# Adding tiles before their sums, turning the heads inside the pointwise product, and starting the convolution beside the second u product

## What is computed

```python
mod = c_act @ ada_w[l] + ada_b[l]                       # 6144 values: shift, scale, gate
h = rms_norm(x, norm_g[l]) * (1 + scale) + shift
z = h @ w_in[l]
q_lat, kv_lat, k_rope, mla_gate, conv_in, conv_gate = split(z)      # 512, 256, 64, 1024, 2048, 1024
q  = rms_norm(q_lat)  @ w_q_up[l]                       # 8 heads of 128 + 64
kv = rms_norm(kv_lat) @ w_kv_up[l]                      # 8 heads of 128 + 128
q, k = rms_norm over each head, then rope on the last 64 columns (k's 64 are shared by the heads)
mla_out = causal_attention(q, k, v) * silu(mla_gate)
u = u_val * sigmoid(u_gate)                             # from conv_in
u = causal_depthwise_conv(u, dw_w[l], dw_b[l])          # 31 taps, 1024 channels
u = silu(layer_norm(u)) @ w_pw[l] + b_pw[l]
conv_out = u * silu(conv_gate)
x = x + gate * (concat(mla_out, conv_out) @ w_out[l])
```

## Time and profile before

| | us |
|---|---|
| runs, median (lowest to highest) of 3 | 2267.42 (2266.95 to 2269.32) |
| the profiled execution, its own time | 2269.92 |
| its span | 2268.1 |
| PE busy | 2189.5 (97%) |
| DVE busy | 1672.6 (74%) |
| ACT busy | 975.8 (43%) |
| POOL busy | 221.3 (10%) |

### The profile page before, as it was taken

The page is one execution under the profiler, slowest core; times in us unless marked ns, Lnnn a source line. Parts: engine busy times, 40 slices in busy tenths (PEclk is TensorE's granted clock), DMA queues, the critical chain, the costliest instruction groups (busy, mean ns, idle before and its releaser), DMA issues.

```text
span 2268.1 us, 39910 instructions
## 1 busy us (share of the span) xinstructions
PE 2189.5 (97%) x15710; PEld 2081.1 (92%) x15710; DVE 1672.6 (74%) x2302; ACT 975.8 (43%) x1542; POOL 221.3 (10%) x141
## 2 busy tenths in 40 slices
PE   6899999999999999999999999899999999999997
PEld 5899997889999978999999999899999999988886
DVE  4678997698999966977875897787876565653554
ACT  3234436324444363354454345455544444434443
POOL 0000670000006700033000000000000000000000
PEclk8789999999999999999999999999999999999999
DMA  9979867797898587969946997568866555566563
GB/s 353 323 260 329 263 192 258 250 328 269 306 364 258 149 282 247 315 176 294 365 133 224 360 375 240 178 206 273 271 199 209 184 183 179 183 218 186 189 194 121
DMA packets 399194, 560.62 MB, mean 247 GB/s; under 512 B 26043, under 2 KB 317443, under 8 KB 398428
## 3 DMA queue, kind: packets, MB, share of 16 engines
q1 hardware_dynamic: 394496, 550.70, 74.1%
q0 software_dynamic: 1952, 5.37, 0.9%
q10 hardware_dynamic: 2620, 2.83, 0.4%
HBM read 556.64 MB, written 2.21 MB: 246 GB/s over the span
## 4 chain that ended last, share of the span: by engine, by line
PE 87%; DVE 6%; ACT 3%; DMA 2%; issue 2%; ACTq 0%; SPq 0%; DVEq 0%
PE gemm L1956 75%; PE quad L1956 3%; PE gemm L2126 2%; DVE ada_even L1317 1%; PE quad L2081 1%; DVE w_lo L1398 1%; ACT w_hi L909 1%; DMA ada_first<-in_ada_w 1%; DVE ada_odd L1317 1%; DMA w_raw<-in_w_in 1%; PE quad L1980 0%; PE quad L2065 0%; DVE scr L1447 0%; PE quad L1988 0%; PE quad L2126 0%
## 5 line engine op out<-in xcount | busy, mean ns | idle before, releaser
L1956 PE MATMUL gemm<-h_hi,w_hi 128*128 128x256 f32 (+2 forms) x3200 | 912.7, 285 | 12.2 <-DVE h_lo L1452 5.8
L1398 DVE TENSOR_TENSOR w_lo<-w_raw,w_hi 128x1024 fp32r<-128x1024 f32 (+1 forms) x524 | 638.0, 1230 | 381.3 <-ACT w_hi L909 380.2
L1956 PE MATMUL gemm<-h_lo,w_hi 128*128 128x256 f32 (+2 forms) x3200 | 908.2, 284 | 0.0
L1956 PE MATMUL gemm<-h_hi,w_lo 128*128 128x256 f32 (+2 forms) x3200 | 908.0, 284 | 0.0
L909 ACT ACTIVATE w_hi<-w_raw 128x1024 fp32r<-128x1024 f32 (+1 forms) x588 | 607.9, 1046 | 683.2 <-PE gemm L1956 524.7
L1956 PEld LDWEIGHTS gemm<-h_hi,w_hi 128*128 128x128 f32 (+2 forms) x3200 | 614.3, 192 | 15.2 <-issue 9.3
L1956 PEld LDWEIGHTS gemm<-h_lo,w_hi 128*128 128x128 f32 (+2 forms) x3200 | 614.3, 192 | 0.6
L1956 PEld LDWEIGHTS gemm<-h_hi,w_lo 128*128 128x128 f32 (+2 forms) x3200 | 614.3, 192 | 0.3
L1317 DVE SCALAR_TENSOR_TENSOR ada_even<-ada_raw,c_act,ada_even 128x1024 f32<-128x1024 f32 x160 | 215.5, 1347 | 7.0 <-DMA ada_raw<-in_w_ada 3.6
L755 POOL TENSOR_TENSOR w_lo<-w_raw,w_hi 128x1024 fp32r<-128x1024 f32 x64 | 160.8, 2519 | 399.2 <-ACT w_hi L909 399.0
L1317 DVE SCALAR_TENSOR_TENSOR ada_odd<-ada_raw,c_act,ada_odd 128x1024 f32<-128x1024 f32 x128 | 163.7, 1279 | 13.2 <-DMA ada_raw<-in_ada_w 8.5
(11 more groups left out here) (375 smaller groups left out, 3006.0 us busy)
## 6 DMA issues: line engine op xcount, KB each, us to landing
w_raw<-in_w_in SPq DMA_DIRECT2D x264, 512.0 KB, 5.6
w_raw<-in_w_up SPq DMA_DIRECT2D x176, 512.0 KB, 3.6
ada_raw<-in_w_ada SPq DMA_DIRECT2D x160, 512.0 KB, 6.1
ada_raw<-in_ada_w SPq DMA_DIRECT2D x156, 512.0 KB, 6.5
w_raw<-in_w_out SPq DMA_DIRECT2D x96, 512.0 KB, 6.7
w_raw<-in_w_down SPq DMA_DIRECT2D x88, 512.0 KB, 3.7
ada_late<-in_w_ada SPq DMA_DIRECT2D x32, 512.0 KB, 5.1
ada_first<-in_ada_w SPq DMA_DIRECT2D x24, 512.0 KB, 11.5
```

Of the source, the lines that this page charges most:

```text
L1398: dve.tensor_tensor(w_lo[:, fixed % PARTS, 0:sz], w_raw[:, fixed % RAW, 0:sz], w_hi[:, fixed % PARTS, 0:sz].bitcast(F32), ALU.subtract).th ...
L1956: last = pe.matmul(half(g, k, q), left, right, start=(kt == 0 and j == 0 and (q == 0 or g.wide)), stop=(u == len(g.units) - 1 and t == nk ...
```

## The change

- **Sums over added tiles.** The squares of the latents are added in pairs on GpSimd (`lat_added`) and PE sums two tiles in one place, after ua's unit 4. The convolution's tile pairs are added on GpSimd into `conv_sum` (`conv_added`, after cgate's splits), and PE takes the mean from two tiles after kv's unit 2. The squares for the variance are added on DVE from eight tiles to two (`ln_added`), summed after q's unit 2 (`VAR_STEP` 1 to 2, which moves `channel_norm` by one unit on DVE and ACT).
- **Turns.** They go beside pw's units 2 to 7, two groups a unit. There are 12 groups: the rope columns are turned two heads at a time, from new tiles q_rot and k_rot. k's rope columns are scaled and spread by DVE (`k_scale`), ACT scales only the first 128 columns. krT keeps odd heads in its upper half and is zeroed by GpSimd after cgate; it, q_rot and k_rot lie where w_lo is.
- **Convolution.** It starts beside ub: 2 steps a unit there, 3 in gate, 6 in cgate. ub's low parts come from GpSimd; ub is written out as 4 blocks instead of a loop of 2.
- **Pieces.** ub has none. Layer 0: cgate 4, kv 8, q 14, pw 14 (outca, outcb and outm 16, 16 and 8 as before). Layer 1: cgate 4, kv 8, q 8, pw 12. `reduce_mod` of group 5 goes behind pw.

The diff, cut:

```diff
-MEAN_STEPS = (2, 8, 13)
-LAST_MEAN_STEP = 6
-VAR_STEP = 1
+MEAN_STEP = 2
+VAR_STEP = 2
-SPREAD = {"kv": [1] * 6 + [0] * 2, "q": [1] * 4 + [2] * 4, "pw": [1, 1, 1, 0] * 2, "outca": [2] * 8, "outcb": [2] * 8,
-          "outm": [0, 1] * 8}
+SPREAD = [{"cgate": [0] * 12 + [1] * 4, "kv": [1] * 8, "q": [1] * 2 + [2] * 6, "pw": [2] * 6 + [1] * 2,
+           "outca": [2] * 8, "outcb": [2] * 8, "outm": [0, 1] * 8},
+          {"cgate": [0] * 12 + [1] * 4, "kv": [1] * 8, "q": [1] * 8, "pw": [2, 1] * 4}]
+CONV_UNITS = {"ub": 2, "gate": 3, "cgate": 6}
+TURN_STEP = 2
...
-            G["ub", l] = product("ub", wi, 4, CB, full, 2, "a", h_hi, h_lo,
-                                 lambda i, k, B: O_U + 2 * CB + i * CB + (1 - k) * DC, ada=(2, 16, 1) if l == 0 else (3 + 3 * l, 0, 1))
+            G["ub", l] = product("ub", wi, 4, CB, full, 4, "a", h_hi, h_lo,
+                                 lambda i, k, B: O_U + (2 + i * (B // 2) + k // 2) * CB + (1 - k % 2) * DC, by_pool=True)
...
             for l in range(LAYERS):
+                pool.wait_ge(lat_squared, l + 1)
+                link(pool.tensor_tensor(lat_sq[:, 0:2], lat_sq[:, 0:2], lat_sq[:, 2:4], ALU.add))
+                pool.tensor_tensor(lat_sq[:, 0:5:4], lat_sq[:, 0:5:4], lat_sq[:, 1:6:4], ALU.add).then_inc(lat_added, 1)
+                split_low(G["ub", l])
                 split_low(G["gate", l])
                 split_low(G["cgate", l])
-                wait_out(pool, G["pw", l])
-                link(pool.memset(qrT[ROPE:P], 0.0))
-                pool.memset(krT[ROPE:P], 0.0).then_inc(rope_padded, 1)
+                for pair in range(1, CT // 2):
+                    pool.wait_ge(conv_tap, CT * TAPS * l + 2 * TAPS * (pair + 1))
...
+                    pool.tensor_tensor(conv_sum[:], conv[:, 0:2] if pair == 1 else conv_sum[:], conv[:, 2 * pair:2 * pair + 2],
+                                       ALU.add).then_inc(conv_added, 1)
...
+                wait_out(pool, G["cgate", l])
+                link(pool.memset(krT[ROPE:P, 0:NH:2, :], 0.0))
+                pool.memset(krT[0:ROPE, 1:NH:2, :], 0.0).then_inc(rope_padded, 1)
...
-                through(G["gate", l], none, lambda _, v: convolve(range(2 * v, 2 * v + 2)))
-                if l:
-                    mod_out(3 * l + 2)
-                through(G["cgate", l], none, lambda _, v: convolve(range(split + 6 * v, min(split + 6 * v + 6, conv_steps))))
+                through(G["ub", l], lambda i, k: value_of_u(i, k, G["ub", l]), beside_units(done[0], "ub"))
                 wait_out(dve, G["ub", l])
+                through(G["gate", l], none, beside_units(done[1], "gate"))
+                through(G["cgate", l], none, beside_units(done[2], "cgate"))
                 through(G["kv", l])
...
                 rope_tables()
+                dve.wait_ge(ln_squared, l + 1)
+                link(dve.tensor_tensor(ln_sq[:, 0:4], ln_sq[:, 0:4], ln_sq[:, 4:8], ALU.add))
+                dve.tensor_tensor(ln_sq[:, 0:2], ln_sq[:, 0:2], ln_sq[:, 2:4], ALU.add).then_inc(ln_added, 1)
                 k_rotate()
                 through(G["q", l], none, channel_norm)
                 k_scale()
...
-                multiply(G["pw", l], ready=(un_ready, lambda t: CT * l + t))
-                if not l:
-                    reduce_mod(2)
-                wait_out(pe, G["q", l])
-                for b in range(16):
...
+                def turn_heads(_, n, l=l):
+
+                    for b in range(max(2 * (n - TURN_STEP), 0), 2 * (n - TURN_STEP) + 2):
...
+                multiply(G["pw", l], turn_heads, ready=(un_ready, lambda t: CT * l + t))
+                reduce_mod(3 * l + 2)
+                pe.wait_ge(tr_read, QK_TR[l] + QK_GROUPS)
```

More of the change, by code:

```diff
@@ L447, in program @@
                             G_hi, G_lo, lambda i, k, B: (i * B + k) * WB)
[L448 to L458, removed]
+        spread = [[(2, j) for j in range(AU // 2, AU)] + [(n, j) for n in (3, 4) for j in range(AU)],
+                  [(6, j) for j in range(AU)]]
+        for l, pieces in enumerate(spread):
+            for name, counts in SPREAD[l].items():
+                g = G[name, l]
+                g.ada, g.plan = None, []
+                for c in counts:
+                    g.plan.append(pieces[:c])
+                    pieces = pieces[c:]
+                for n, j in sum(g.plan, []):
+                    if j == 0:
+                        g.zero = n
+            assert not pieces
         after = {id(g): n for g, n in zip(prods, prods[1:] + [None])}
@@ L474, in program @@
             if l:
[L475 removed]
+                uses += [f"norm{l}", f"lat{l}", f"mean{l}", f"var{l}", f"mod{2 + 3 * l}", f"mod{3 + 3 * l}"]
             else:
@@ L1676, in q_rotate @@
                            [rope_tab[:, 0, j].unsqueeze(2).to_broadcast([P, TT, NH, HALF]) for j in range(4)],
-                           [ropet[:, j] for j in range(4)]).then_inc(qk_ready, 1)
+                           [ropet[:, j] for j in range(4)], q_rot[:, :, :, 0:HALF], q_rot[:, :, :, HALF:ROPE]).then_inc(qk_ready, 1)
                 def q_root(l=l):
@@ L2196, in _ @@
                 pe.wait_ge(lat_ready, l + 1)
-                if l:
-                    reduce_mod(3 * l + 2)
                 multiply(G["gate", l])
-                def mean(pair, l=l):
-                    if pair == 0:
-                        stat_write(pe, f"mean{l}")
-                    pe.wait_ge(conv_tap, CT * TAPS * l + 2 * TAPS * (pair + 1))
-                    for c in (2 * pair, 2 * pair + 1):
-                        last = pe.matmul(stat[:, 0:T], ones[:], conv[:, c, :], start=(c == 0), stop=(c == CT - 1))
-                    if pair == CT // 2 - 1:
-                        last.then_inc(stat_ready, 1)
@@ L2210, in _, with mean @@
-                multiply(G["cgate", l], lambda _, n: mean(MEAN_STEPS.index(n)) if n in MEAN_STEPS else None)
+                def mean(_, n, l=l):
+                    if n == MEAN_STEP:
+                        pe.wait_ge(conv_added, (CT // 2 - 1) * (l + 1))
+                        summed(f"mean{l}", [conv_sum[:, c, :] for c in range(2)])
+                multiply(G["cgate", l])
                 pe.wait_ge(lat_ready, l + 1)
-                multiply(G["kv", l], lambda _, n: mean(CT // 2 - 1) if n == LAST_MEAN_STEP else None)
+                multiply(G["kv", l], mean)
@@ L2214, in variance @@
                 def variance(_, n):
                     if n == VAR_STEP:
-                        pe.wait_ge(ln_squared, l + 1)
-                        summed(f"var{l}", [ln_sq[:, c, :] for c in range(CT)])
+                        pe.wait_ge(ln_added, l + 1)
+                        summed(f"var{l}", [ln_sq[:, c, :] for c in range(2)])
                 multiply(G["q", l], variance)
-                multiply(G["pw", l], ready=(un_ready, lambda t: CT * l + t))
-                if not l:
-                    reduce_mod(2)
@@ L2236, in _ @@
-                pe.wait_ge(tr_read, QK_TR[l] + 16)
+                def turn_heads(_, n, l=l):
+                    for b in range(max(2 * (n - TURN_STEP), 0), 2 * (n - TURN_STEP) + 2):
+                        if b == 0:
+                            wait_out(pe, G["q", l])
+                        if b == 4:
+                            pe.wait_ge(k_scaled, l + 1)
+                        if b == 8:
+                            pe.wait_ge(qk_ready, l + 1)
+                        if b == 10:
+                            pe.wait_ge(k_rope_ready, l + 1)
+                        dst = tr_bank(QK_TR[l] + b)
+                        for j in range(2):
+                            for t in range(TT):
+                                if b < 8:
+                                    x = (q_tok, k_tok)[b // 4][:, t, 2 * (b % 4) + j, 0:NOPE]
+                                else:
+                                    pair = 2 * (b % 2) + j
+                                    x = (q_rot, k_rot)[b // 2 % 2][:, t, 2 * pair:2 * pair + 2, :].rearrange("p h d -> p (h d)")
+                                last = pe.transpose(dst[:, j * T + t * P:j * T + (t + 1) * P], x, ident[:])
+                        last.then_inc(tr_ready, 1)
@@ L2242, in scores @@
                         pe.matmul(o, qnT[:, h, t * P:(t + 1) * P], knT[:, h, 0:keys], start=True, stop=False)
-                        last = pe.matmul(o, qrT[:, h, t * P:(t + 1) * P], krT[:, h, 0:keys],
+                        last = pe.matmul(o, qrT[:, h // 2, t * P:(t + 1) * P], krT[:, h, 0:keys],
                                          start=False, stop=True)
```

91 lines of the change are left out of this document (51 added, 40 removed).

## The result

Median 2248.98 us (2248.17 to 2250.07, 4 runs) against 2267.46 (2266.95 to 2269.32, 4 runs): ratio 0.9923, 95% interval 0.9911 to 0.9934, 18.5 us less. The forecast was 2250.0. The profiled execution has a span of 2247.1, which is 21.0 less than before; 2.4 of that lie in the unchanged start (ua begins at 150.86 for 153.22), where the runs scatter. The change itself is therefore read stage by stage.

The account below looks back on a forecast made before the run. TensorE was taken as the bound. Gains of 13.8 (sums), 8.1 (turns) and 6.6 (kv), less 10.7 (stall) and 0.4 (pw's end), gave 17.4 us gained: 2250.0 us from a median of 2267.42, range 2238 to 2262.

Parts of the forecast that it names:

- Step 1: Variance, mean and latent sums over added tiles, both layers: fewer PE records, 13.8 us gained, the adds on GpSimd hidden.
- Step 2: Head turns moved inside pw: the wait behind pw goes, 4.5 and 3.6 us by layer, 8.1 us gained.
- Step 3: Convolution begun beside ub, GpSimd at 2.40 us per unit: it ends before kv, layer 0's kv loss goes, 6.6 us gained.
- Step 4: Late channel_norm and q_out(2) stall pw 6.8 us in layer 0, 1.3 in layer 1; with clock, 10.7 us lost.
- K+19.4: Time after kv's end (K) when layer 0's eight pieces ahead of channel_norm were to be done.
- The clock term: Half clock behind layer 0's stall at pw, priced from the earlier kv gap: 2.6 us more.
- Step 5: Rest of pw: DMA is tight, pw_out(3) comes just late at pw's end, 0.4 us lost.
- rival (a): No stall at pw in either layer: 28.5 us gained, 2238.9 us; chance 0.19.
- Rival (c): GpSimd, blocked by DVE pieces, becomes the bound of ub: 26 us over 32 units, 2276 us; chance 0.03.
- The forecast's two prices for one size: GpSimd adds of 128x512: 1.2 us each if cost goes by size, 2.4 if not; hidden either way.

Follow-up runs that it names:

- x8: Changed kernel without VectorE's adds of the squares, the variance summed over eight tiles on TensorE: 2245.9 us.
- x10: x5 without VectorE's adds of the squares, the variance summed over eight tiles on TensorE: 2244.0 us.
- x7: Kernel before the change, with four instead of six pieces beside kv and two more beside outm: 2260.3 us.
- x1: Changed kernel, layer 0's 14 q pieces reordered so that two instead of eight stand ahead of channel_norm: 2249.3 us.
- x5: Changed kernel, eight of layer 0's pieces back beside ub, and two instead of eight ahead of channel_norm: 2240.4 us.
- x11: x5 with layer 1's q pieces also put behind channel_norm, as [1,1,0,0,0,2,2,2]: 2239.1 us.
- x6: Changed kernel, layer 0 with sixteen pieces beside ub, one per unit, none beside cgate, and q and pw replanned: 2246.6 us.
- x2: Changed kernel with VAR_STEP back from 2 to 1, taking two pieces from ahead of channel_norm in layer 0: 2252.8 us.
- x9: x5 with its eight q pieces ahead of channel_norm again, the transfers otherwise the same: 2250.0 us.

## Why the prediction was right

The sum, 17.4, came within 1.1 us of the medians' difference, 18.5. That is nearer than the terms are: the two layers gave 16.2, and 2.3 came from elsewhere, which is luck. Layer 1's sum, 9.2, was met by 9.1. Layer 0's, 8.2, was met by 7.0, with misses of both signs: the clock (1.1), the stall (0.3) and pw's end (0.4) came cheaper, waits of 1.7 and 0.8 were not priced, and 0.5 stays unplaced. Step by step:

- **Step 1 (sums).** As forecast in records: 4, 4 and 8 (0.95 us). But "2.6 us on PE" for the variance is worth that only where pw does not wait. In layer 0 it bought a longer stall (x8); x10 shows 2.6 where it counts.
- **Step 2 (turns).** 8.1 forecast; undoing the place costs 8 to 10, 3.3 of it clock. They hide, apart from 0.78 us at the second group, where the ring waits for ACT.
- **Step 3 (convolution, GpSimd).** Kv lost its idle, GpSimd kept 2.40, the convolution ended 18.6 us before kv (forecast 20). The cause of the kv loss was read rightly, and x7 shows it; that the early convolution was needed to remove it was wrong.
- **Step 4 (stall).** 6.8 forecast, 6.49 measured; 1.3 against 0.95 in layer 1; both put down to q_tok as forecast. Channel_norm came 2 us later than K+19.4, q_out(2) began at K+28.3 and was over at K+30.4 for K+28.4: late pieces waited 2.6 us for DMA where I gave 0.5. The stall did not grow by it, since q itself ended later (pw could have begun at K+23.9, not K+21.6). The clock term, 2.6, measured 1.5. I had sized it from the gap in kv, whose loss behind the idle was 2.6.
- **Missed.** Waits for q's weights, 1.7 us: I had SP stand behind the fifth piece until K+9, had q's last weights behind it, and gave that no price. SP's rows show the stand, from 350.80 to 361.38:

```profile
347.55 2.61 SPq L698 DMA_DIRECT2D ada_raw<-in_ada_w  x2
350.20 0.60 SPq L711 DMA_DIRECT2D w_raw<-in_w_q_up  x1
361.38 1.93 SPq L698 DMA_DIRECT2D ada_raw<-in_ada_w  x2
```

- **Step 5.** The 0.4 at pw's end did not come, and by x8 the same bytes land in time for an outca 4.6 us sooner. Still, late transfers were the more important point: rival (a), "no stall", was weighed as if only the chain stood against it, while x1 shows that without the pile the weights of pw can take its place. x5 and x11 come near its 2238.9 (2240.4, 2239.1) with both changed.

Rival (c) fell in the changed kernel, since ub's DVE work is taps; x6 shows that it holds with a piece in every unit, at 6 us.

## What to carry to other kernels

When a stall is found, ask what is late next within the length of the stall before giving its whole length to the one cause: here the chain and late weights were within 1 us of each other in the plans tried, and removing either gave nothing, while removing both gave 9 us. Then look for what stands ahead of both: taking VectorE's wait from the head of the chain made layer 0 4.6 us shorter without moving a piece. A matmul taken off PE is worth its time only if what replaces it is not at the head of the chain that PE waits for next. And a table of "which piece goes beside which unit" decides more than the arithmetic does: two pieces moved gained 7 us in the old kernel, and eight moved gained 9 in the new one.

## What the runs showed of the hardware

- The granted clock fell behind some gaps and not behind others. PE idle for 2.73 us between dense units left the next unit at 3.72 us (x2), 2.13 at 3.69 (x1); a 3.62 us gap made it 6.42, and 2.08 us after a row of spaced turns made it 5.26. The same idle of 6.5 us ahead of pw cost 1.5 us of clock in the changed kernel and 2.8 in x9. So the length of a gap alone does not give its price; what else decides is not shown.
- A DVE piece with two SBUF inputs (1.28 us alone) and a GpSimd subtraction (2.40 beside taps) shared a unit in x6: the piece took 1.85, the subtraction a mean of 3.25, and the pair came round every 3.35 us, not every 3.7 as one strictly behind the other would.
- GpSimd's adds of 128x512: the first of the latent pair took 1.29 us in layer 0, with VectorE idle beside it, and the second 2.36, beside a split and a piece on VectorE; the convolution's took 2.27, and 4.33 for two, beside pieces. The forecast's two prices for one size, 1.2 and 2.4, both occurred.
